# Token-major keys and values for an HGRN2 layer: block transposes on VectorE with on-chip transfers, in place of TensorE transposes

## What is computed

```python
b = jnp.cumsum(gi, axis=2)              # log decay inside a chunk
qe = qi * jnp.exp(b)
ke = ki * jnp.exp(-b)
inter = jnp.einsum('bhck,bhkv->bhcv', qe, S)
A = jnp.where(mask, jnp.einsum('bhck,bhsk->bhcs', qe, ke), 0.0)
intra = jnp.einsum('bhcs,bhsv->bhcv', A, vi)
S_new = jnp.exp(bl)[..., None] * S + jnp.einsum('bhsk,bhsv->bhkv', ki * jnp.exp(bl - b), vi)
```

## Time and profile before

| | us |
|---|---|
| runs (3) | 2479.34, 2477.33, 2480.98 |
| the profiled execution's own time | 2479.22 |
| its span in the trace | 2477.4 |
| PE busy | 2448.9 (99% of the span) |
| VectorE (DVE) busy | 1715.5 (69%) |
| ScalarE (ACT) busy | 1294.4 (52%) |

### The profile page before, as it was taken

The page is one execution under the profiler, slowest core; times in us unless marked ns, Lnnn a source line. Parts: engine busy times, 40 slices in busy tenths (PEclk is TensorE's granted clock), DMA queues, the critical chain, the costliest instruction groups (busy, mean ns, idle before and its releaser), DMA issues.

```text
span 2477.4 us, 51670 instructions
## 1 busy us (share of the span) xinstructions
PE 2448.9 (99%) x19353; PEld 2422.5 (98%) x19353; DVE 1715.5 (69%) x2895; ACT 1294.4 (52%) x2203; POOL 178.0 (7%) x210
## 2 busy tenths in 40 slices
PE   9999999999999999999999999999999999999998
PEld 7999999999988999999999999999999999999997
DVE  7776677777688777777676776453586776677677
ACT  4455555555456666666666665221434555555553
POOL 0011111111130000000000000000200111111110
PEclk9999999999999999999999999999999999999999
DMA  3345555555631222112322226423113555555555
GB/s 125 120 107 125 124 122 119 119 125 122 156 147 38 77 69 86 60 60 69 121 78 93 85 72 219 148 95 120 35 53 112 124 122 121 124 123 124 124 124 188
DMA packets 78567, 271.08 MB, mean 109 GB/s; under 512 B 8320, under 2 KB 12800, under 8 KB 77952
## 3 DMA queue, kind: packets, MB, share of 16 engines
q1 hardware_dynamic: 55424, 185.11, 21.7%
q0 software_dynamic: 23040, 84.55, 18.0%
HBM read 154.86 MB, written 114.77 MB: 109 GB/s over the span
## 4 chain that ended last, share of the span: by engine, by line
PE 91%; DVE 4%; DMA 2%; ACT 2%; issue 1%; SPq 0%; ACTq 0%; DVEq 0%
PE banks L149 29%; PE banks L150 29%; PE banks L151 28%; DMA x_sum<-f_part 1%; DMA raw<-w_slabs 1%; DVE mix_blk_lo L502 1%; PE banks L1779 1%; PE banks L1753 1%; PE banks L1723 1%; PE banks L1739 1%; PE banks L1749 1%; PE banks L1747 0%; DVE mix_blk_f L478 0%; ACT mix_blk_hi L494 0%; ACT mix_u_hi L1386 0%
## 5 line engine op out<-in xcount | busy, mean ns | idle before, releaser
L149 PE MATMUL banks<-f_blk_hi,f_u_hi 128*128 128x258 f32 x2496 | 707.1, 283 | 3.2 <-DVE f_blk_lo L502 2.5
L150 PE MATMUL banks<-f_blk_lo,f_u_hi 128*128 128x258 f32 x2496 | 706.4, 283 | 0.0
L151 PE MATMUL banks<-f_blk_hi,f_u_lo 128*128 128x258 f32 x2496 | 705.5, 283 | 0.0
L149 PE MATMUL banks<-mix_blk_hi,mix_u_hi 128*128 128x258 f32 x1808 | 519.6, 287 | 2.9 <-DVE mix_blk_lo L502 1.8
L150 PE MATMUL banks<-mix_blk_lo,mix_u_hi 128*128 128x258 f32 x1808 | 511.6, 283 | 0.0
L151 PE MATMUL banks<-mix_blk_hi,mix_u_lo 128*128 128x258 f32 x1808 | 510.7, 282 | 0.0
L149 PEld LDWEIGHTS banks<-f_blk_hi,f_u_hi 128*128 128x128 f32 x2496 | 472.1, 189 | 5.0 <-issue 2.7
L151 PEld LDWEIGHTS banks<-f_blk_hi,f_u_lo 128*128 128x128 f32 x2496 | 471.9, 189 | 0.0
L150 PEld LDWEIGHTS banks<-f_blk_lo,f_u_hi 128*128 128x128 f32 x2496 | 471.7, 189 | 0.1
L149 PEld LDWEIGHTS banks<-mix_blk_hi,mix_u_hi 128*128 128x128 f32 x1808 | 342.7, 190 | 5.7 <-DVE mix_blk_lo L502 2.6
L150 PEld LDWEIGHTS banks<-mix_blk_lo,mix_u_hi 128*128 128x128 f32 x1808 | 342.5, 189 | 1.0 <-issue 0.2
(11 more groups left out here) (287 smaller groups left out, 4395.1 us busy)
## 6 DMA issues: line engine op xcount, KB each, us to landing
raw<-w_slabs SPq DMA_DIRECT2D x220, 512.0 KB, 3.5
x_sum<-f_part POOLq DMA_DIRECT2D x126, 516.0 KB, 7.8
x_sum<-f_snap POOLq DMA_DIRECT2D x18, 516.0 KB, 10.0
x_sum<-x POOLq DMA_DIRECT2D x16, 516.0 KB, 5.6
x<-x_sum SPq DMA_DIRECT2D x16, 516.0 KB, 8.0
sg_kept<-sgt SPq DMA_DIRECT2D x8, 1032.0 KB, 5.9
sgs<-sg_kept SPq DMA_DIRECT2D x16, 516.0 KB, 4.7
x<-x_t SPq DMA_DIRECT2D x8, 516.0 KB, 8.5
```

The costliest lines, as they stand in the source:

```text
L149: pe.matmul(out, wh, xh, start=start, stop=False, skip_group_check=chained)
L150: pe.matmul(out, wh, xl, start=False, stop=False, skip_group_check=chained)
L151: return pe.matmul(out, wl, xh, start=False, stop=stop, skip_group_check=chained)
```

## The change

Keys: VectorE transposes each 32x32 block of `ke[:, 0:1024]`, in one instruction on contiguous operands, into `f`, which is free by then (`turn_keys`). This leaves each block at its own place, so sixteen DMAs, one for each pair of a band of 32 rows and a band of 32 columns, carry the blocks to their mirrored places in `kt`, which now holds all eight tiles (`move_keys`). Values go in two halves of 512 columns, each with one block transpose and sixteen DMAs. Their staging buffer is `ss` (first half) and `b` (second half); for head 0 it is `b` twice. Only the 8 samples' columns are still turned by PE. Every run of a DMA is 32 numbers, 128 bytes.

```diff
+BAND = 32
+BANDS = P // BAND
+MOVED = 16 * BANDS * BANDS
...
+def turn_keys(dve, k, s, j):
+    dve.wait_ge(s.ke_ready, j * 1 + 1)
+    turn(dve, s.f[:, 0:SEQ], s.ke[:, 0:SEQ]).then_inc(s.key, 1)
...
+def turn_values(dve, k, s, j, h, first=False):
+    if first:
+        dve.wait_ge(s.first_used, 9)
+    elif h:
+        dve.wait_ge(s.taken, one_of(j, 1))
+    else:
+        dve.wait_ge(s.mixed, three_of(j, 1, 1))
+        dve.wait_ge(s.ss_stored, j * 16)
+    if first or h:
+        dve.wait_ge(s.qe_ready, j * 1 + 1)
+    turn(dve, turned_values(s, h, first), s.vb[:, h * HALF_SEQ:(h + 1) * HALF_SEQ]).then_inc(s.values_turned, 1)
...
+def move(sp, to, of, done):
+    bands = [slice(n * BAND, (n + 1) * BAND) for n in range(BANDS)]
+    tiles = of.rearrange("p (n d) -> p n d", d=P)
+    for rows in bands:
+        for cols in bands:
+            sp.dma_start(to[rows, :, cols], tiles[cols, :, rows]).then_inc(done, 16)
...
 def core_tensor(pe, k, s, h, n):
     def chunk_keys(n):
         tok = slice(n * P, (n + 1) * P)
-        wait(pe, s.kt_used, h * 8 + n)
-        last = pe.transpose(k.bank[4][:, 0:P], s.ke[:, tok], k.ident[:, :])
...
     def updates(n):
-        pe.wait_ge(s.kt_used, h * 8 + (n + 1))
-        if n >= 2:
-            pe.wait_ge(s.u_used, h * 8 + (n - 1))
+        if n == 0:
+            pe.wait_ge(s.kt_moved, h * MOVED + MOVED)
+        if n in (0, 4):
+            pe.wait_ge(s.v_moved, h * (2 * MOVED) + (n // 4 + 1) * MOVED)
+        if n >= 1:
+            pe.wait_ge(s.u_used, h * 8 + n)
...
 def core_turn(pe, k, s, j, first=False):
...
-    pe.transpose(k.bank[5][0:DEC, 0:P], s.vb[:, SEQ:T], k.ident[:, :]).then_inc(s.vt_ready, 1)
-    for n in range(TILES):
-        last = pe.transpose(k.bank[6 + n // 4][:, (n % 4) * P:(n % 4 + 1) * P], s.vb[:, n * P:(n + 1) * P],
-                            k.ident[:, :])
...
+    pe.transpose(k.bank[4][0:DEC, 0:P], s.ke[:, SEQ:T], k.ident[:, :])
+    pe.transpose(k.bank[4][0:DEC, P:2 * P], s.vb[:, SEQ:T], k.ident[:, :]).then_inc(s.samples_turned, 1)
...
 def mid_sync(sp, k, s):
     sp.wait_ge(s.prod, PLAIN)
+    move_keys(sp, k, s, 0)
+    for h in range(2):
+        move_values(sp, k, s, 0, h, first=True)
     load_states(sp, k, s, 0)
     for row in range(2):
         load_row(sp, k, s, 1, 1, row)
```

More of the change, by code:

```diff
@@ L44 @@
 NVEC = 15
+BAND = 32
+BANDS = P // BAND
+HALF_SEQ = SEQ // 2
+MOVED = 16 * BANDS * BANDS
 DEC_ROWS = 72
@@ L1642, in plain_vector @@
     queries(dve, k, s, 0, first=True)
+    turn_keys(dve, k, s, 0)
+    for h in range(2):
+        turn_values(dve, k, s, 0, h, first=True)
     lows(T2)
@@ L1807, in core_scalar @@
                        scale=s.el[:, m:m + 1]).then_inc(s.u_used, 1)
[L1808 to L1815, removed]
-    if n == 0:
-        act.wait_ge(s.v_ready, h * 3 + 1)
-        act.activation(s.vst[DEC_LOW_KEYS, :], s.v[0:DEC, TILES, :], ACT.Copy)
-        act.activation(s.vst[DEC_HIGH, :], s.v[0:DEC, TILES, :], ACT.Copy).then_inc(s.vm_ready, 1)
-    if n == 2:
[L1821 to L1831, removed]
+    if n == 0:
+        act.wait_ge(s.samples_turned, h * 1 + 1)
+        act.activation(s.samples_f[0:DEC, :, :].rearrange("p a d -> p (a d)"), k.bank[4][0:DEC, 0:2 * P], ACT.Copy)\
+            .then_inc(s.vm_ready, 1)
+        act.wait_ge(s.vm_ready, h * 4 + 1)
+        act.activation(s.vst[DEC_LOW_KEYS, :], s.samples_f[0:DEC, 1, :], ACT.Copy)
+        act.activation(s.vst[DEC_HIGH, :], s.samples_f[0:DEC, 1, :], ACT.Copy).then_inc(s.vm_ready, 1)
+    if n == 2:
+        act.activation(s.kst[DEC_LOW_VALUES, :], s.samples_f[0:DEC, 0, :], ACT.Copy)
+        act.activation(s.kst[DEC_HIGH, :], s.samples_f[0:DEC, 0, :], ACT.Copy).then_inc(s.sample, 1)
 def core_vector(dve, k, s, h, n):
@@ L1927, in load_states, with move_keys, move_values @@
 def load_states(sp, k, s, h):
-    wait(sp, s.ss_stored, h * 16)
+    if not (isinstance(h, int) and h == 0):
+        sp.wait_ge(s.v_moved, h * (2 * MOVED) + MOVED)
     sp.dma_start(s.ss[:, :, :].rearrange("p b d -> p (b d)"),
                  k.state_hgrn[bass.ds(h, 1)].rearrange("a p c -> p (a c)")).then_inc(s.ss_loaded, 16)
+def move(sp, to, of, done):
[4 more added lines that the diff above has]
+            sp.dma_start(to[rows, :, cols], tiles[cols, :, rows]).then_inc(done, 16)
+def move_keys(sp, k, s, h):
+    sp.wait_ge(s.key, h * 2 + 2)
+    move(sp, s.kt, s.f[:, 0:SEQ], s.kt_moved)
+def move_values(sp, k, s, j, h, first=False):
+    if first and h:
+        sp.wait_ge(s.v_moved, MOVED)
+    sp.wait_ge(s.values_turned, j * 2 + (h + 1))
+    move(sp, s.v[:, h * (TILES // 2):(h + 1) * (TILES // 2), :], turned_values(s, h, first), s.v_moved)
 def store_out(sp, k, s, h):
@@ L3008, in build @@
     k.mid.s_out = r.put("s_out", [P, P], F32)
-    k.mid.kt = [r.put(f"kt{n}", [P, P], F32) for n in range(2)]
+    k.mid.kt = r.put("kt", [P, TILES, P], F32)
     k.mid.sgt = Region(gates_at, end).put("sgt", [P, 2, T], F32)
```

64 lines of the change are left out of this document (35 added, 29 removed).

## The result

| | us |
|---|---|
| before, median of 4 runs | 2478.54 |
| after, median of the runs | 2611.42 |
| ratio | 1.0538 (95% interval 1.0526 to 1.0550) |
| predicted | 2509 (2474 to 2572) |
| span of the profiled execution after | 2609.0 (before 2477.4) |

The change is slower by 133 us. The direction was right; the size lies outside the range.

A forecast was written before the change was run, and what follows sets the result against it. PE was taken as the bound, with issues on the SP queue as the largest new cost: 2479.2 us plus 15 over seven steady groups plus 15 in group 1 gives 2509 us, range 2474 to 2572.

The forecast's parts named there:

- What bounds the kernel: Whole kernel: PE, busy for 99% of the span, so time is won only on PE or in its waits.
- the keys at the first update: Steady group: the last key transfer lands at 884.4, PE wants it at 882.85, so PE waits 1.55 us.
- PE's gain: Each head: sixteen transposes at 0.11 us and a wait of 0.39 go, 2.15 us a head, 15 us over seven groups.
- VectorE's new work: Each head: block transposes take 2.35 us, covered by waits, slack and idleness, so costed at nothing.
- I take p = 0.44 us from issue to issue: SP queue, 48 transfers a head: time from one issue to the next, bounds 0.33 and 0.60.
- The three rows: Issues before: 0.33 us with one contiguous run per partition, 0.40 with four, 0.47 with two from a strided source.
- the 0.15 us of slack: Steady group, VectorE's sums for PE's fifth score: the part of the slab's 2.85 us lateness that costs nothing.
- the 2.7 us: Steady group: PE's further wait because the slab of row 1 lands late behind the second value half.
- rival 3: DMA engines become the bound at 40 ns a packet, 2 us of clock lost in group 1: 2540 us, chance 0.22.
- steady group: Waits of 1.55 and 2.7 us less 2.15 gained: 2.1 us lost a group, 15 us over seven.
- Group 1: No earlier group to issue in; the slab of row 0 lands late, PE's third update starts at 793.0: 15 us lost.
- Rival 4: SP issues at 0.60 us: waits of 6.5 and 5.4 a group, 23 in group 1, 2570 us, chance 0.09.

The follow-up runs named there:

- the probe: Changed kernel plus 45 further transfers in group 8, 15 forms of three each, to price an issue by form; its total time means nothing.
- the best version here: Changed kernel with 8 transfers a set through DRAM, whole keys, SP's loop written out and the core one half later: 2484.63 us, 1.0026 of the kernel before.

## Why the prediction was off

- **What bounds the kernel, and the direction: right.** PE is the bound, and the change made it wait at the two places named: the keys at the first update, and VectorE at `mix_sum` for the slab that stands behind the transfers.
- **PE's gain: right.** 2.15 us a head predicted, 2.08 in the run with one transfer a set.
- **VectorE's new work costs nothing: right.** 1.15 and 0.6 us from start to start were taken for the block transposes; they last 1.24 and 0.70, with 1.16 and 0.63 to the next instruction, and PE is never idle where only the transfers are cheap.
- **The step that failed: "I take p = 0.44 us from issue to issue".** It is 0.65 to 0.69 (0.60 to 0.61 for the issue itself), above even the upper bound of 0.60. The three rows it rests on were taken as if the number of runs set the price, and the run with large packets shows that it does not: 0.59 us with a single run a partition. None of the three rows has SBUF at both ends, which costs 0.16 us more in the probe for the change's own pattern. And the row of the trace before that has the right price, L1280 at 0.61, was not among them. What sets the price of an issue stays open.
- **How it grows.** With 48 issues a head, 0.21 us more each is 10 us of queue. By the prediction's own sums p = 0.65 gives 8.1 us at the first update in place of 1.55 (measured 8.7 on average, 9.3 at most) and 6.2 behind the slab in place of 2.7. VectorE does wait about that long for the slab (5.33 us in the row shown, 6.2 at most), but PE only 2.9 to 3.1: after the long stall at the keys VectorE is further ahead of PE than the 0.15 us of slack that were taken. So the 2.7 us came out near by luck, with the slab later and the slack larger than forecast.
- **The second fault: the forecast had no term for the clock.** It stood only in rival 3, at 2 us a group. PE's busy time in a steady period is 56.5 us on average against 51.7 in the run with one transfer a set, for the same work: 4.8 us a group. Over the whole execution it is 2469.0 against 2435.9 us, 33 us, a quarter of the loss.
- **The sum again, for a steady group:** idle time +11.9, clock +4.8, less work of PE -1.7, together +15.0 as measured on average over five periods, where +2.1 was predicted. Group 1: about 26 in place of 15, with PE's third update at 801.38 in place of the forecast 793.0 and ScalarE 14.45 us at the split in place of 8 to 12.
- **Rival 3 (the DMA engines): fell.** Large packets in as many transfers changed nothing measurable (2608.2 against 2611.4 us, intervals of the ratios overlapping), and as many small packets in a quarter of the transfers cost no steady wait. The Trainium skill's rule that small descriptors are read, modified and written ("DMA: Bandwidth & Descriptors", Specifications) shows no cost within SBUF here; its rule that transfers under 64 KB should be merged (same page, Rules for kernel authors) is borne out by the runs with 4 and 1 transfers a set.
- **Rival 4 (0.60 us): nearest.** Its mechanism is what happened, at a price a little higher and with the clock on top. It had 0.09. The chance was too small for a price that a row of the trace before already had.

## What to carry over

- Before moving work from an engine to transfers, count the issues, and look at every row of the queue for the price of one, not only at the three that seem like it in shape. No row had the same two ends here; the price was then open upwards, and the dear end of the range deserved more than a chance of 0.09.
- A queue is an engine in program order: 48 issues at 0.65 us, with four transfers between them, held it for 34 us, where the whole group had taken 54, and moving the slabs ahead of the transfers that did not need to come first won back a third of the loss.
- A stall of the bounding engine costs clock as well: 2.1 us a group with 9.9 us of idleness, and another 2.7 with the second stall of 3 us; price both. And where a move has no earlier group to hide in, its whole latency is paid once (12 us of waits in the best version here).

## What the hardware showed that was not expected

- The issue of a transfer from SBUF to SBUF on SP lasts 0.47 us for 128 partitions of one contiguous run (0.52 in the probe), 0.51 for 32 partitions of one 128-byte run, 0.59 for 32 runs of 0.5 to 1 KB, 0.60 to 0.69 for 128 to 1024 short runs, and 0.82 to 1.48 for the three of L2445. With DRAM at one end it is 0.32 to 0.38 in the kernel with 5 transfers a set, 0.30 to 0.45 in the probe, 0.61 for L1280 in the trace before, and 0.58 to 0.73 in the kernel with 8. The number of runs does not explain that alone: 128 runs of 512 bytes were stored at 0.33 to 0.38 in the one and loaded at 0.60 in the other. The law was not settled.
- GpSimd issues in 0.55 us (0.63 for the stores through DRAM), but stands still for 1.5 to 5.2 us every few transfers; the trace does not say for what.
- PE's load of weights whose elements lie 16 or 32 bytes apart lasts 330 to 335 ns in place of 190, and a block transpose of 1024 columns written with its elements 32 bytes apart 2220 in place of 1239.
